# Output and query projections in token parts of 416 and 128 columns instead of two parts of 272

## The reference, cut to what matters

```python
mix = jnp.concatenate([ya, yb], axis=-1) @ lp['w_out']           # output projection, 2048 x 2048
x = _layernorm(ALPHA * x + (1 + g1) * mix, lp['ln1_w'], lp['ln1_b'])
h2 = x * (1 + sc2) + sh2
# inside _peer(h2, ...):
q = (xb @ w_q).reshape(PEER_BLOCK, P_HEADS, 2, D_QH)             # query projection, 2048 x 2048
s1 = jnp.einsum('thd,kd->thk', q[:, :, 0], sub_keys[0])          # scores, top-16, gates
...
act = jax.nn.gelu(jnp.einsum('thkd,td->thk', peer_u[e], xb))     # 16384 experts, 16 of them per head
return jnp.einsum('thk,thkd->td', gate * act, peer_v[e])
```

## Time and profile before

| | us |
|---|---|
| median of two runs | 5163.99 |
| profiled execution | 5167.61 |
| its span | 5166.0 |
| TensorE busy | 4722.0 (91%) |
| VectorE busy | 2815.5 (55%) |
| ScalarE busy | 1153.3 (22%) |
| GpSimd busy | 876.1 (17%) |

### The profile page before, as it was taken

How to read it: one execution, slowest core, us unless ns; L and a number is a source line. 1 busy time by engine, 2 the same in 40 slices (tenths; PEclk the granted TensorE clock), 3 DMA queues, 4 the chain that set the end, 5 groups by cost and what they waited for, 6 DMA issues and landing times. The chain is left out here.

```text
span 5166.0 us, 69332 instructions
## 1 busy us (share of the span) xinstructions
PE 4722.0 (91%) x27980; PEld 4294.1 (83%) x27980; DVE 2815.5 (55%) x4159; ACT 1153.3 (22%) x1511; POOL 876.1 (17%) x634
## 2 busy tenths in 40 slices
PE   9897898898899967987999999999989999999997
PEld 7676677677677756976999999999979999999996
DVE  0333342443443443345990676766767777777775
ACT  0132111111111111122222322222222222222222
POOL 0000011111111111004355321211111111111110
PEclk9998998898898878997999999999989999999998
DMA  8221111121122112312234788888877777777773
GB/s 297 87 68 64 64 64 67 65 72 67 57 72 67 39 51 69 149 69 73 82 128 138 256 306 296 285 298 296 288 253 264 267 247 277 267 255 270 267 258 135
DMA packets 203578, 864.84 MB, mean 167 GB/s; under 512 B 19968, under 2 KB 108160, under 8 KB 112256
## 3 DMA queue, kind: packets, MB, share of 16 engines
q1 hardware_dynamic: 91104, 530.35, 29.0%
q0 software_dynamic: 40192, 277.37, 15.1%
q10 hardware_dynamic: 72096, 54.54, 3.2%
HBM read 791.71 MB, written 70.48 MB: 167 GB/s over the span
## 5 line engine op out<-in xcount | busy, mean ns | idle before, releaser
L88 PE MATMUL PS<-first_HH,tail_WH 128*128 128x416 f32 (+1 forms) x3072 | 1029.1, 335 | 43.5 <-DVE first_HL L1470 31.4
L90 PE MATMUL PS<-first_HH,tail_WL 128*128 128x416 f32 (+1 forms) x3072 | 1020.8, 332 | 0.0
L89 PE MATMUL PS<-first_HL,tail_WH 128*128 128x416 f32 (+1 forms) x3072 | 1014.0, 330 | 0.0
L88 PE MATMUL PS<-dn_BH,tail_WH 128*128 128x416 f32 x2048 | 730.9, 357 | 65.4 <-DVE dn_BL L1986 44.4
L90 PE MATMUL PS<-dn_BH,tail_WL 128*128 128x416 f32 x2048 | 724.0, 353 | 0.0
L89 PE MATMUL PS<-dn_BL,tail_WH 128*128 128x416 f32 x2048 | 717.5, 350 | 0.0
L88 PEld LDWEIGHTS PS<-first_HH,tail_WH 128*128 128x128 f32 x3072 | 580.9, 189 | 48.6 <-issue 40.4
L89 PEld LDWEIGHTS PS<-first_HL,tail_WH 128*128 128x128 f32 x3072 | 581.6, 189 | 6.2
L90 PEld LDWEIGHTS PS<-first_HH,tail_WL 128*128 128x128 f32 x3072 | 579.5, 189 | 3.1
L88 PEld LDWEIGHTS PS<-dn_BH,tail_WH 128*128 128x128 f32 x2048 | 385.2, 188 | 96.7 <-issue 63.1
L701 PE MATMUL PS<-mix_HT,mix_RING 128*128 128x276 f32 x1536 | 376.8, 407 | 49.9 <-DMA mix_RING<-in_w_in 24.9
(11 more groups left out here) (351 smaller groups left out, 6405.2 us busy)
## 6 DMA issues: line engine op xcount, KB each, us to landing
tail_WR<-in_peer_u SPq DMA_DIRECT2D x128, 1024.0 KB
tail_WR<-in_peer_v SPq DMA_DIRECT2D x128, 1024.0 KB
mix_RING<-in_w_ada SPq DMA_DIRECT2D x96, 1024.0 KB, 4.8
mix_RING<-in_w_in SPq DMA_DIRECT2D x42, 1024.0 KB, 4.9
tmp_z<-up_ZB ACTq DMA_DIRECT2D x128, 208.0 KB
tmp_gd<-up_STG ACTq DMA_DIRECT2D x26, 1024.0 KB, 9.3
dn_GG<-tmp_gd SPq DMA_DIRECT2D x16, 1664.0 KB, 7.9
dn_ZI<-tmp_z SPq DMA_DIRECT2D x128, 208.0 KB, 2.4
```

The source lines that it names most:

```text
L88: nc.tensor.matmul(out, r32(wh), r32(xh), start=first, stop=False)
L89: nc.tensor.matmul(out, r32(wh), r32(xl), start=False, stop=False)
L90: return nc.tensor.matmul(out, r32(wl), r32(xh), start=False, stop=last)
```

## The change

The table of token parts becomes 0 to 416 and 416 to 544. The copies out of PSUM follow it: VectorE's of the output tile read columns 0 to 416 from the first bank and the other 96 prompt tokens and 32 sample tokens from the second; ScalarE's of the query tile are two instead of three, because the first part now ends where the first place in `QT` ends. Nothing else is edited.

```diff
-PARTS = ((0, TH), (TH, T))
+PARTS = ((0, TD), (TD, T))
...
-                    V.tensor_scalar(tmp[:, 0:TH], ps[:, 0, 0:TH], gate[:, 0:1], None, ALU.mult)
-                    V.tensor_scalar(tmp[:, TH:SEQ], ps[:, 1, 0:SEQ - TH], gate[:, 0:1], None, ALU.mult)
-                    V.tensor_tensor(samples4(tmp[:, SEQ:T]), samples4(ps[:, 1, SEQ - TH:TH]), bcast(gate[:, 1:9], 2, NS),
-                                    ALU.mult)
+                    V.tensor_scalar(tmp[:, 0:TD], ps[:, 0, 0:TD], gate[:, 0:1], None, ALU.mult)
+                    V.tensor_scalar(tmp[:, TD:SEQ], ps[:, 1, 0:(SEQ - TD)], gate[:, 0:1], None, ALU.mult)
+                    V.tensor_tensor(samples4(tmp[:, SEQ:T]), samples4(ps[:, 1, (SEQ - TD):TS]), bcast(gate[:, 1:9], 2, NS), ALU.mult)
...
-                A(QT[:, i % 2, 0:TH], PS[:, 2 * (i % 2), 0:TH], ACT.Copy)
-                A(QT[:, i % 2, TH:TD], PS[:, 2 * (i % 2) + 1, 0:TD - TH], ACT.Copy)
-                A(QT[:, i % 2, 4 * P:5 * P], PS[:, 2 * (i % 2) + 1, TD - TH:TH], ACT.Copy).then_inc(q_ready, 1)
+                A(QT[:, i % 2, 0:TD], PS[:, 2 * (i % 2), 0:TD], ACT.Copy)
+                A(QT[:, i % 2, 4 * P:5 * P], PS[:, 2 * (i % 2) + 1, 0:TS], ACT.Copy).then_inc(q_ready, 1)
```

## The result

The changed kernel takes **5239.88 us** (median of two runs, 5239.57 and 5240.18) against 5163.99 us before: a ratio of 1.0146 with a 95% interval of 1.0130 to 1.0163. It is 76 us slower, a clear difference, but under 2%.

What follows compares the result with a forecast made beforehand. TensorE's matmul stream was taken to bound both projections; 31 tiles x 2.39 us + 1 us = 75 us on the profiled 5167.6 us gave 5242.6, on the median's scale 5239 us, with a range of 5230 to 5414 us.

Steps and rivals of the forecast that it cites:

- PE bounds both stages: Output and query projections: TensorE is busy nearly throughout, so each nanosecond put on their matmul stream arrives at the end.
- The wide matmuls: Projection tiles: 48 matmuls per tile grow from 272 to 416 columns, from 125.6 to 188.9 ns each, +63.3 ns.
- The narrow matmul: Projection tiles: 48 matmuls per tile shrink to 128 columns and cost their weight load, 112 ns (ends 108 and 126).
- The 81 ns: Skill page's figure per load and matmul pair at 128 columns; by it the change costs 29 us; not used.
- Per tile: Each of 16 output and 16 query tiles grows by 48 x 49.7 ns = 2.39 us.
- The sum: Both projections: 31 tiles x 2.39 us, plus 1 us for the first output tile, is 75 us.
- No wait moves: Whole kernel: no wait, semaphore or transfer is added or moved; next weights' loads only come later with the split.
- slack: VectorE's routing gets scores 2 x 2.4 us per head later; 132 us of slack makes the price zero, otherwise up to 4.8.
- The copies: ScalarE's query tile copies fall from 0.97 to 0.81 us, VectorE's output tile instructions keep their sum; effect on time: nothing.
- A: Narrow matmuls in the projections run by columns at 62 ns, loads not binding; time stays at 5164 us; chance 0.08.
- C: The 48 narrow matmuls of each tile lose their single pass, 224 ns each; 247 us more, 5411 us; chance 0.20.
- D: Clock falls in the projections' narrow parts, a load taking 0.16 to 0.17 us; 84 us more, 5323 us; chance 0.10.

Runs made afterwards that it cites:

- half_weights: The changed kernel with half the weights in the narrow part (64 of 128 output channels, the others left out): 5158.8 us.
- out_only: The changed kernel with parts of 416 and 128 columns only in the output projection, the query projection as before the change: 5199.6 us.
- three_copies: The changed kernel with four ScalarE copies of a query tile instead of two, each copy cut in half: 5235.3 us.
- interleave: The changed kernel, same parts of 416 and 128 columns, with wide and narrow matmuls alternating: 5232.6 us.
- parts_320_224: The changed kernel with its cut moved, parts of 320 and 224 columns instead of 416 and 128: 5173.3 us.
- query_only: The changed kernel with parts of 416 and 128 columns only in the query projection, the output projection as before the change: 5201.4 us.

## Why the prediction was right

The forecast was 5239 us for the measured 5239.88. By its steps:

1. *PE bounds both stages.* Right: all of it arrived at the end, and each projection alone brought its half.
2. *The wide matmuls* at 188.9 ns, right: 0.19 us in the loads above.
3. *The narrow matmul* at 112 ns, right: 111. The 112 came from one pair of loads of this product and from rows of plain matmuls. half_weights shows that the load makes it, which the prediction had only argued. The 81 ns of the Trainium skill, "TensorE: Matmul & The Clock Gate", section "Back-to-back issue gap", were not seen in any run here with full loads of this type: by them the time would have been 5193 us.
4. *Per tile* 2.39 us was forecast; the two periods grew by 2.41 and 2.38.
5. *The sum* of 75 us: right in size, and closer than its terms. From the first matmul of the output projection to the first of the experts it was 2587.08 - 2071.18 = 515.9 us (2587.08 is in the earlier trace rows, 2071.18 is the start behind the longest wait of the earlier trace rows) and is 2659.63 - 2070.24 = 589.4 us now, 73.5 more. The first two output tiles, up to the first mean group, grew by 1.0 us (33.6 to 34.7) where 1 + 2.39 were forecast: their waits took up part of the growth, and the granted clock over them was 0.93 instead of 0.82. The other 14 output tiles brought 33.7. Then comes a price that the forecast put at nothing: the norm between the two projections took 1.2 us more, since the clock over its first 14 us was 0.79 instead of 0.89; out_only and three_copies have 0.79 and 0.80 there, and interleave, which has no row of 48 narrow matmuls, 0.89 as before. The query tiles, up to the last score group, brought 37.2 where 16 x 2.39 = 38.2 were forecast. The first expert tile, also unforecast, ran at half clock for 3.4 us, some 1 us more; three_copies and parts_320_224 show a dip there too, while query_only, with the same query stage, and interleave do not, so it does not hang on the parts alone. The span grew by 72, the stages ahead and behind being some 3 us shorter with nothing in them changed. That 5239 met the median to 1 us is luck: these errors of 1 to 2.4 us cancel in part, and the interval of the ratio leaves 67 to 84 us open.
6. *No wait moves.* Right. The routing had slack to spare: VectorE's last step of it waits 168.3 us for ScalarE now, had 132. I had it wrong that scores which come later in each head would eat this slack. The ScalarE step behind expert tile 28 moved by 74 us, but the end of the routing only by 38 (2721.8 to 2759.4), of which 35 are the later start of the query stage. In query_only, where that stage alone is longer, the routing ended 2.6 us later. VectorE works through its own backlog there, and later scores hardly delay it.
7. *The copies* are worth nothing: right, by three_copies. ScalarE's take 517 and 271 ns instead of the earlier trace rows's three.

Of the rivals, A (loads don't bind) and C (224 ns) are ruled out by the changed kernel's own loads. D was the nearest: at 128 columns the clock stayed at 1.00 inside both stages and dipped only behind them, at 96 it fell in part of the tiles. My chance of 0.10 for it was not too high. Its price was built wrongly, though near in size: I took 0.16 us for a load at half clock from the first two loads of a stage and let it hold for all narrow matmuls. In the runs such a load took 0.21 us, the wide matmuls at half clock paid too, and the clock was low for a part of the time only; together that was 85 and 104 us with 64 and 32 columns, where I had 84.

## What to carry to other kernels

Price a matmul by the longer of its weight load and its columns: here, with 128 x 128 weights of this type, 111 ns against about 6 ns + 0.44 ns a column, so any cut with both parts at 240 columns or more cost the same (272 and 272, 304 and 240), and a part below that threw the difference away. Alternating wide and narrow matmuls did not help: a pair still took 0.30 us, as if only one load could run ahead. And when the matmuls of a part get narrower, look at the granted clock of the stage, and of what follows it, and not at the busy share, which was 100% at either clock.

## What the runs showed of the hardware

- The granted clock fell to half in a stream that never waited, in the runs with 48 matmuls in a row of 96, 64 or 32 columns (0.91 to 0.82 over the two stages), and not inside the stages of those with 48 of 128 or more. It cost some 47 to 104 us in those runs.
- Behind the last 48 matmuls in a row of 128 columns and full weights the granted clock was lower: 0.79 to 0.80 in the first 14 us of the norm in the three runs with them in the output projection (the change, out_only, three_copies), against 0.89 in the kernel before; it cost 1.2 us.
- Alternating 512 and 32 columns, the clock stayed at half for 63 and 64 us from the start of the two stages of unbroken matmuls, and once up it stayed up for 249 and 248 us in the same pattern.
- A load of 64 weight columns let matmuls follow each other every 60 ns, one of 128 every 111 ns.
